# The mLSTM read-out and its product by token halves, and the last group of the down projection by token halves with its norm and the stores beside it

## The reference

```python
def mlstm_readout(h, o, norm_g, w_out):          # h = h_forward + h_backward
    hn = h * lax.rsqrt(jnp.mean(h * h, axis=-1, keepdims=True) + EPS)
    hn = hn * norm_g.astype(jnp.float32).reshape(H, 1, M_DV)
    hn = hn.transpose(0, 2, 1, 3).reshape(B, T, H * M_DV)
    y = (hn * jax.nn.sigmoid(o.astype(jnp.float32))).astype(o.dtype)
    return y @ w_out

def conv_ffn(h, up_w, conv_w, conv_b, down_w, on_grid):
    u, g = jnp.split(h @ up_w, 2, axis=-1)
    g = dwconv3(g.reshape(B, rows, GRID_W, F), conv_w, conv_b, axis=2).reshape(B, T, F)
    return (jax.nn.silu(g) * u) @ down_w

    yx, yc = mlstm_mixer(hx, hc, m_in_w[j], m_in_b[j], m_norm_g[j], m_out_w[j], ctx_out)
    x = x + g1[..., None, :] * rmsnorm_2(yx, post_mix_g[i])
    hx = modulate(rmsnorm_2(x, pre_ffn_g[i]), sh2, sc2)
    yx = conv_ffn(hx, ffn_up_w[i], ffn_conv_w[i], ffn_conv_b[i], ffn_down_w[i], True)
    x = x + g2[..., None, :] * rmsnorm_2(yx, post_ffn_g[i])
```

## Time and profile before

| what | value |
|---|---|
| median of three runs | 2344.55 us |
| time of the profiled execution | 2347.46 us |
| its span, first to last instruction | 2345.6 us |
| TensorE matmul busy | 2157.1 us (92%), 9876 instructions |
| TensorE weight load busy | 1785.9 us (76%) |
| VectorE, ScalarE, GpSimd busy | 1103.7 us (47%), 774.6 us (33%), 671.8 us (29%) |
| mean granted TensorE clock | 0.951 of full speed |
| DMA | 245.19 MB, mean 105 GB/s |

### The profile page before, as it was taken

One profiled execution on the slowest core, in us unless ns is written; L12 is line 12 of the kernel. 1 busy time (PEld: TensorE's weight loads), 2 busy tenths in 40 slices (PEclk: granted clock), 3 DMA queues, 4 the chain that ended last, 5 costly groups with the idle time before them and its releaser, 6 DMA issues.

```text
span 2345.6 us, 26000 instructions
## 1 busy us (share of the span) xinstructions
PE 2157.1 (92%) x9876; PEld 1785.9 (76%) x9876; DVE 1103.7 (47%) x1039; ACT 774.6 (33%) x884; POOL 671.8 (29%) x308
## 2 busy tenths in 40 slices
PE   5999799997999999999979957979999999999995
PEld 4788687876878787888859946747888888887874
DVE  7689988777333656412236652082222222412124
ACT  4333254564342332122334443232222222302122
POOL 1466455544222221211201124402222222222240
PEclk7999999999999999999989977979999999999997
DMA  9431111221212333356578852121112122123211
GB/s 364 169 128 45 30 59 60 64 68 45 72 59 79 123 90 120 104 172 212 171 200 235 224 200 85 54 72 54 45 45 80 57 77 80 54 72 117 67 59 72
DMA packets 280109, 245.19 MB, mean 105 GB/s; under 512 B 7714, under 2 KB 251523, under 8 KB 280035
## 3 DMA queue, kind: packets, MB, share of 16 engines
q1 hardware_dynamic: 270355, 234.75, 32.5%
q10 hardware_dynamic: 9680, 9.44, 1.2%
HBM read 196.12 MB, written 48.04 MB: 104 GB/s over the span
## 4 chain that ended last, share of the span: by engine, by line
PE 41%; issue 38%; DVE 10%; POOL 6%; DMA 3%; ACT 2%; SPq 0%; POOLq 0%; ACTq 0%; DVEq 0%
PE PS L1372 31%; POOL wl L678 5%; DVE PS L1835 5%; PE PS L1641 1%; PE PS L1649 1%; PE PS L1642 1%; PE PS L1675 1%; PE PS L1528 1%; DVE SCR L1749 1%; DMA B<-rows_d 1%; PE PS L1615 1%; DMA SCR<-in_ctx 1%; PE PS L1635 1%; PE PS L1621 1%; PE PS L1634 1%
## 5 line engine op out<-in xcount | busy, mean ns | idle before, releaser
L1372 PE MATMUL PS<-XH,wh 128*128 128x512 f32 x2448 | 762.9, 393 | 28.9 <-POOL wl L678 18.3
L678 POOL TENSOR_TENSOR wl<-raw,wh 128x1024 fp32r<-128x1024 f32 (+2 forms) x177 | 415.6, 2348 | 1248.0 <-ACT wh L865 1026.1
L1372 PE MATMUL PS<-XL,wh 128*128 128x512 f32 x2448 | 759.1, 391 | 0.0
L1372 PE MATMUL PS<-XH,wl 128*128 128x512 f32 x2448 | 758.4, 391 | 0.0
L1372 PEld LDWEIGHTS PS<-XH,wh 128*128 128x128 f32 x2448 | 460.9, 189 | 133.3 <-POOL wl L678 16.3
L1372 PEld LDWEIGHTS PS<-XL,wh 128*128 128x128 f32 x2448 | 462.5, 189 | 96.9
L1372 PEld LDWEIGHTS PS<-XH,wl 128*128 128x128 f32 x2448 | 462.4, 189 | 96.9
L1835 DVE SCALAR_TENSOR_TENSOR PS<-B,PJ,PS 128x1022 f32<-128x1022 f32 (+7 forms) x197 | 251.1, 1274 | 7.5
L865 ACT ACTIVATE wh<-raw 128x1024 fp32r<-128x1024 f32 (+1 forms) x120 | 125.4, 1045 | 312.4 <-PE PS L1372 245.8
L2246 DVE SCALAR_TENSOR_TENSOR SCR<-SCR,PV 128x1008 f32<-128x1008 f32 x22 | 28.0, 1271 | 256.6 <-ACT SCR L1308 256.6
L939 ACT ACTIVATE wh<-raw 128x1024 fp32r<-128x1024 f32 (+1 forms) x56 | 54.1, 965 | 268.5 <-PE PS L1372 232.8
(11 more groups left out here) (337 smaller groups left out, 2440.7 us busy)
## 6 DMA issues: line engine op xcount, KB each, us to landing
B<-in_ada_w SPq DMA_DIRECT2D x48, 512.0 KB, 6.0
raw<-in_ffn_up_w SPq DMA_DIRECT2D x44, 512.0 KB, 4.1
raw<-in_w_in SPq DMA_DIRECT2D x40, 512.0 KB, 3.8
raw<-in_m_in_w SPq DMA_DIRECT2D x29, 512.0 KB, 5.2
proj_d<-B SPq DMA_DIRECT2D x17, 512.0 KB, 3.0
mod_tiles<-in_mod_w SPq DMA_DIRECT2D x16, 512.0 KB, 13.0
raw<-in_w_out SPq DMA_DIRECT2D x16, 512.0 KB, 4.3
B<-proj_d SPq DMA_DIRECT2D x8, 1024.0 KB, 6.5
```

The lines of the kernel that those rows point to most:

```text
L678: tt(wl[slot][:, 0:kc, :], raw[slot][:, 0:kc, :], wh[slot][:, 0:kc, :].bitcast(F32), ALU.subtract).then_inc(lo_done, 1)
L1372: last = mm(ps[:, c:c + step_n], W[:, k, :], Y[:, k, c:c + step_n], start=(seen == 0), stop=(seen == total - 1))
```

## The change

It makes these edits.

- **Read-out in the recurrence.** The strips are taken in the order 3, 4, 2, 5, 1, 6, 0, 7 (`ORDER`), the order in which both directions have them. The read-out of the first four is put between the last steps of the recurrence, on every engine (`readout`). The last chunk of each direction no longer transposes k, makes kw or updates C (`is_final`). The gate strips are loaded by SP instead of ScalarE's queue. The sum strips lie in `ctx_memory`.
- **G5 by token halves.** 16 half tiles of 24 matmuls: two tiles over the first 512 tokens in two steps of 256, six more over the first 512, then eight over the second 512. Every half tile has its own weight unit, so each unit is loaded and split twice. The transposes of strips 4 to 7 stand before the half tiles 3 and 5. The norms of the first 512 tokens stand between the half tiles 8 to 15.
- **G6's first four tiles by token halves.** Tiles 0 and 1 of the first half open piece by piece, with the sums of the second half in between, then tiles 2 and 3, then the same for the second half. Both sums of squares go through GpSimd and token sums, so that the reciprocal over 1024 columns is gone.
- **Last group of G7 by token halves.** 16 half tiles of 18 matmuls, the first two interleaved (`AHEAD_K = 3`). The norm of the first half, its scaling and the transposes and stores of four strips stand between the half tiles of the second half; the second half is scaled in two steps of 256 tokens.
- **First block.** `ada_load` issues four loads with each unit instead of three. In the last round ScalarE calls SiLU once on a spare number and does `ls_evac` ahead of the square root.

```diff
-                for n in range(3 * (U - 3), min(3 * (U - 2), (1 + EARLY) * KD)):
+                for n in range(3 + 4 * (U - 4), min(3 + 4 * (U - 3), (1 + EARLY) * KD)):
                     ada_load(n)
...
+            for n in range(4):
+                gate_load(n)
+            for j in range(NT - 4, NT - 2):
+                for d in range(2):
+                    h_store(j, d)
+                    chunk_load(j + NC + 2, d, j % 2)
+                for n in range(2):
+                    read_load(2 * (j - NT // 2) + n)
+            for t in range(2, 4):
+                half_unit(t)
             for j in range(NT - 2, NT):
                 for d in range(2):
                     h_store(j, d)
...
+            for n in range(4, NT):
+                sp.wait_ge(*at("xl_r", n - 3))
+                if n == 4:
+                    for d in range(2):
+                        sp.wait_ge(*at(f"h_out{d}", 16 * NT))
+                read_load(n)
+            for n in range(4, NT):
+                gate_load(n)
+            for n, c in enumerate(ORDER):
+                sp.dma_start(B2[:, :, P * n:P * (n + 1)], x2_d.rearrange("(k p) t -> p k t", p=P)[:, :, P * c:P * (c + 1)]).then_inc(ev(f"x2_in{n // 4}"), 16)
+            for t in range(4, 2 * KD):
+                half_unit(t)
...
+            X_SUMS = {10: (0, 3), 11: (3, 6), 12: (6, KD)}
+            for t in range(2 * KD - 1):
+                half_low(t + 2)
+                y_sum(t)
...
+                for k in range(*X_SUMS.get(t, (0, 0))):
+                    x_sum(0, k)
...
                 if last:
+                    f(spare[:], eps[:], ACT.Silu)
+                    ls_evac(i)
                     hi(ls_unit(i) + 2)
                     for k in range(DVE_HIGH, KD - 2):
                         lru_high(k)
...
             lru_high(KD - 2)
-            ls_evac(KD - 1)
             lru_high(KD - 1)
...
+            def y_evac(t):
+                high_at(G5.U + 2 + t, 0)
+                b, h = (G5.T + t) % 2, t // KD
+                act.wait_ge(unit_used, G5.U + t + 3)
...
+                f(part(B1[:, t % KD, :], h), part(PS[b], h), ACT.Copy).then_inc(ev("y_sb"), 1)
+                act.wait_ge(*at("yssq_ok", t + 1))
+                f(part(ysq_t, h), part(PS[b], h), ACT.Square).then_inc(ev("ysq_ok"), 1)
...
+            def x_square(h, k):
+                n = KD * h + k
+                act.wait_ge(*at(f"x3_sb{h}", k + 1))
+                act.wait_ge(*at("xssq_ok", max(n, 1)))
+                f(part(xsq_t, k % 2), part(B2[:, k, :], h), ACT.Square).then_inc(ev("xsq_ok"), 1)
...
+            y_evac(KD + 2)
+            for k in range(2, 5):
+                x_square(0, k)
+            y_evac(KD + 3)
+            for k in range(5, KD):
+                x_square(0, k)
...
+            def half_tile(g, t, ps, h):
+                pe.wait_ge(lo_done, g.U + t + 3)
+                for k in range(KD):
+                    last = piece(ps, (g.U + t) % 2, None, k, HALF * h, HALF)
+                last.then_inc(unit_used, 1)
...
+            for t in range(2, 2 * KD):
+                if t in (3, 5):
+                    for n in range(2):
+                        read_transposes(t + 1 + n)
+                if t == KD:
+                    pe.wait_ge(*at("xl_r", NT))
+                elif t == KD + 1:
+                    pe.wait_ge(*at("yssq_ok", KD + 1))
+                    half_sums(PS[2], part(ysum_t, 0), event="n2_ps0")
+                elif t == KD + 2:
+                    half_stat("n2", PS[2], part(T[4], 0), 0)
+                elif t == KD + 6:
+                    pe.wait_ge(*at("xssq_ok", KD + 1))
+                    half_sums(PS[3], part(xsum_t, 0), event="n3_ps0")
+                elif t == KD + 7:
+                    half_stat("n3", PS[3], part(T[4], 1), 0)
+                b = (G5.T + t) % 2
+                pe.wait_ge(taken[b], (G5.T + t) // 2 + 1)
+                half_tile(G5, t, PS[b], t // KD)
...
+            AHEAD_K = 3
+            for k in range(LAST_KC + AHEAD_K):
+                if k < LAST_KC:
+                    if k == 0:
+                        last_begin(0)
+                    pe.wait_ge(*at("xl_G7", down[LAST][0] + k + 1))
+                    last_piece(0, k)
+                if k >= AHEAD_K:
+                    if k == AHEAD_K:
+                        last_begin(1)
+                    last_piece(1, k - AHEAD_K)
```

More of the change, by code:

```diff
@@ L372, in recurrence, with is_final @@
             if step:
-                step.done(NT // 2 - 1)
-            for u in range(4):
-                pair(NCH // 2 - 1, u, True, True, u < 3)
+                step.done(NT // 2 - 2)
+            for w in range(8):
+                pair(NCH // 2 - 2 + w // 4, w % 4, True, True, w < 7)
+                if readout:
+                    readout(w)
+        def is_final(x):
+            return isinstance(x, int) and x >= 2 * NCH - 2
         def indices(k, slot, d):
@@ new lines, in readout, with piece @@
+            def readout(w):
+                for n in {5: (0,), 6: (1,), 7: (2, 3)}.get(w, ()):
+                    read_transposes(n)
+            recurrence(pe, transposes, heads, readout=readout)
+            def piece(ps, w, X, k, c, n):
+                for m, (W, Y) in enumerate(((wh[w], XH), (wl[w], XH), (wh[w], XL))):
+                    last = mm(ps[:, c:c + n], W[:, k, :], Y[:, k, c:c + n], start=(k == 0 and m == 0), stop=(k == KD - 1 and m == 2))
+                return last
+            def half_tile(g, t, ps, h):
+                pe.wait_ge(lo_done, g.U + t + 3)
+                for k in range(KD):
+                    last = piece(ps, (g.U + t) % 2, None, k, HALF * h, HALF)
+                last.then_inc(unit_used, 1)
@@ new lines, in half_opening @@
+            def half_opening(g, t, pss, h, ready, between={}):
+                pe.wait_ge(lo_done, g.U + t + 4)
+                for k in range(KD):
+                    if k in between:
+                        between[k]()
+                    pe.wait_ge(*at(ready, KD * h + k + 1))
+                    for s in range(2):
+                        last = piece(pss[s], (g.U + t + s) % 2, None, k, HALF * h, HALF)
+                        if k == KD - 1:
+                            last.then_inc(unit_used, 1)
@@ L1673, in _ @@
                     for k in range(KD):
-                        for n, (W, Y) in enumerate(((wh[w], XH), (wl[w], XH), (wh[w], XL))):
-                            last = mm(ps[:, half * c:half * (c + 1)], W[:, k, :], Y[:, k, half * c:half * (c + 1)],
-                                      start=(k == 0 and n == 0), stop=(k == KD - 1 and n == 2))
+                        last = piece(PS[b], (G5.U + s) % 2, None, k, 2 * P * c, 2 * P)
                     if c == 1:
                         last.then_inc(unit_used, 1)
-            tiles(G5)
```

724 lines of the change are left out of this document (429 added, 295 removed).

## The result

Four runs of the changed kernel took 2317.35 to 2322.83 us, median **2319.65**; the kernel before has by now four runs with the median 2346.22. The ratio is 0.9887, 95% interval 0.9871 to 0.9903: faster by 1.1%, 26.6 us, where 52 were forecast. The time lies 1.65 us above the range.

What follows compares the result with a forecast made beforehand. TensorE, busy 92% of the span, bounds the kernel, so only its waits and low-clock stretches can pay. Terms -13.9 - 6 - 26 - 6.3 = -52.2 us: profiled 2295.3, median 2292, 8-in-10 range 2268 to 2318.

Steps and rivals of the forecast that it cites:

- The prediction's own sign of being wrong: Recurrence longer by more than 8 us; listed beside no DMA-bound stall at half tile 4 and TensorE idle in every half tile.
- First block: Four loads a unit close the 11.73 us hole before the first gates: -13.9 us, range -8 to -15.
- the 12.4: First block: part of VectorE's 14.3 us of waits for modulation weights that four loads a unit take off.
- ls out of PSUM: First block's end: ls copied ahead of the square root, so the next product's opening ends sooner: -6 us, range -3 to -8.5.
- Recurrence +7.8, less 4: Recurrence: strip sums and a norm add 7.8 us; final chunks without state products and k transposes save 4.
- Half tile 4: G5: its weights queue behind strips, gates and x2 on SP, so TensorE stalls 11 us.
- rival 1: G5: weights of half tile 4 don't wait, so the stall of 11 us goes: 2281 us, 20%.
- The other half tiles: G5's other 12: 65.3 us, plus 2.1 transposes, 3.7 first norm, 2.5 lower clock, 10 stalls; half tile 15 ends at 1510.
- Last group: G7's last group: last matmul 11.8 us later, the tail behind it 18.1 shorter: -6.3 us, range 0 to -12.
- Rival 2: New stages stall more: read-out 6 us, GpSimd and ScalarE lockstep 8, last group gains nothing (+6): 2312 us, 20%.
- Rival 3: First block's edits give nothing because another wait takes the place at once: 2311 us, 4%.
- Rival 4: Supply of half-tile weights becomes the bound in G5, G6's halves and the last group: +87 us, 2379 us, 4%.

Runs made afterwards that it cites:

- e1: Kernel before with the first block's two edits alone (four loads a unit; ls copied ahead of the square root): 2331.39 us against 2349.03, ratio 0.9929.
- e2: Changed kernel with the sums of both directions of the strips one step later in the recurrence: 2308.60 us, ratio 0.9833 to the kernel before.
- e4: Changed kernel with the eight loads of x2 put one by one behind the weights of half tiles 4 to 11: 2304.62 us, ratio 0.9815.
- e5: Changed kernel with x3's sums of squares on VectorE instead of GpSimd: 2311.00 us, ratio 0.9842 to the kernel before.
- e3: Changed kernel with half tile 0 of the last group whole ahead of half tile 1 (AHEAD_K = 6 instead of 3): ratio 0.9882.
- e9: Changed kernel, strip sums one step later, x2 behind weights, x3 sums on VectorE, AHEAD_K = 6, earlier unit 1 copy, later gate loads: 2289.90 us, ratio 0.9744.

## Why the prediction was wrong

The direction was right, and every place that it named was a real one. It was wrong by its size, 27.7 us: 22.2 from the spans (52.2 forecast, 30.0 seen), and 5.2 from the median, which I set 2.9 below the profiled time as in the kernel before, while it lies 2.3 above it now. The 22.2 are 11.7 up to G5's start, 8.5 from there to G6's tile 4, 0.7 behind it and 3.1 in the last group, less 1.8 that the first block gave too much in this execution. The prediction's own sign of being wrong, a recurrence longer by more than 8 us, came true.

- **First block: the mechanisms right, the size by luck.** e1 puts both edits at -16.7 (-13 to -20), a little under the forecast -19.9; the -21.7 here are those of one early execution. In it modulation sums end at 140.6 (139.6 was forecast by the 12.4) and the hole is gone, -13.8 for the forecast -13.9. ls out of PSUM gave -7.9 rather than -6, by the end of the first chunk's opening at 569.8 (591.5 before), inside its range: the late pieces of XL held TensorE less than I charged. As ScalarE's timeline shows, no drain was added either:

```profile
542.02 1.28 ACT L1108 ACT_TABLE_LOAD   x1
543.31 0.20 ACT L1108 ACTIVATE spare<-eps 128x1 f32<-128x1 f32 x1
543.42 1.01 ACT L1051 ACTIVATE B<-PS 128x1024 f32<-128x1024 f32 x1
```

  The first operation behind the table load runs 0.01 us after its end. The Trainium skill's figure of about 1.38 us of drain ("ScalarE: Activation LUTs", What ACT_TABLE_LOAD costs) does not show here; the measurement decides.
- **Recurrence: the step that failed.** "Recurrence +7.8, less 4" came out at +24.9, since it priced the waits for the strips and not the work put into the chain, nor the clock that TensorE loses behind each stop. The first term's arithmetic, 15.1 us from a store to its sum, was right (15.3, from the store issued at 1298.0 to the sum at 1313.28). But I let the sum stand 10.8 behind the store where it stands 9.2, and I counted the wait alone: the second strip's wait (1.55) and the two sums' own 2.5 are on the same chain, 9.9 in all for 4.3. The later steps cost 0.8, 8.2 (two waits of together 4.0, a wait of 2.60 for ScalarE, whose squares of the sum strips stand ahead of its exponentials, and three operations of 1.2), 3.3 and 3.1, where I had 0.6 and 2.9 and then a gain of 4. What saved 9 of these 21 us: from the last normaliser to G5 it was 5.9 us where the forecast had 15.1 (1387 less 1368.05 and 3.8), as most of the read-out had by then been done. Net, G5 was 11.8 late, and e2 gives 12.4 of it back.
- **Half tile 4: right.** 10.06 for 11, from 40.5 us after G5's start for 39.5. The queue's bytes were the reason, as e4 shows; rival 1 (no wait, 20%) falls. The terms of its sum add up to 1427.3 and not 1426.5, which changes nothing here.
- **The other half tiles: the stalls right, the clock behind them too small.** I named GpSimd's 7.5 against 5.44 and ScalarE behind it, and took 10 of 0 to 20; the waits are 3.80 and 5.89. e5 gives 10.3 back in G5 by that edit alone. From half tile 4 to the end of half tile 15 it took 88.0 for 83.6, though: the sum has 2.5 for the lower clock behind the first stall and nothing behind the others, where the granted clock was 0.77 from 1476 to 1505.6. On to G6's tile 4 it was 79.1 for 75.5.
- **Last group: the tail right, the head wrong.** From the last matmul to the end 28.6 for 29.7. The head took 83.5 for 79.3: I priced the wait for unit 1 as if most of half tile 0 were finished under it. With `AHEAD_K = 3` only three pieces of it are there to do, so the other three stood behind the wait too, at a granted clock of 0.64 over the first 18.5 us. e3 and its like give back 3 to 4.
- **Rivals.** Rival 2 (2312) is nearest to what happened: the read-out held G5 back by 11.8 instead of 6, the stretch to G6's tile 4 took 8.6 more, and half of the last group's gain was lost instead of all. But the 8.6 are not the dearer lockstep that it named: the stalls are as taken, and the clock and G6's opening are what was dearer. Rival 3 falls by e1. Rival 4 needed 7.3 us a half tile throughout; splits as far apart as that (9.4) are in the rows only where GpSimd had sums to do as well.

## What to carry to other kernels

Work that is put between the steps of a chain costs on the chain everything that it executes there, besides what it waits for, and what TensorE loses in clock behind each stop; before it is moved in, count all three, and put a sum that needs a transfer one whole step later than the transfer's sum of durations says. Where bytes are added to a queue, ask of each load when its first reader comes: loads that nobody reads for 60 us belong behind the weights that are read in 20. And before the large part of a change is written, measure the small edits beside it alone; here they held two thirds of the gain.

## What the runs showed of the hardware

A stall costs more than its length: behind the 10.06 us before half tile 4 TensorE came back at 1.2 GHz (0.43 us from matmul to matmul of 512 columns for 0.23, a granted clock of 0.52 in the first 3.9 us), which made it some 12. In e9 the difference was greater still: with an idle stretch of 6.18 us instead of 4.79 in the recurrence the matmuls behind it took 4.1 us more. Moving the same 4.2 MB on one queue from ahead of a unit of weights to behind it took that whole wait away without any other wait for x2. And executions of the same first part of the program differed by up to 6 us in when the mLSTM started, while the stage behind it agreed within 0.4 us (188.5, 188.3 and 188.1 to G5 in three kernels, 200.9 to 201.1 in the changed kernel and four variants). The last group, at the other end, differed by 1.7 us with its code unchanged.
